# The recurrent mixer's input projection as three products of split weights and split input

## The reference

```python
def _recurrent_mixer(h, w_in, conv_w, conv_b, ga_w, ga_b, gx_w, gx_b, lam, w_out):
    u = h @ w_in                                   # 256x1024 by 1024x2048
    gate = jax.nn.gelu(u[..., :LRU_WIDTH])
    rec = _causal_depthwise_conv(u[..., LRU_WIDTH:], conv_w, conv_b)   # 4 taps
    rec = _rg_lru(rec, ga_w, ga_b, gx_w, gx_b, lam)
    return (gate * rec) @ w_out
```

## Time and profile before

| | |
|---|---|
| median of 3 runs | 1732.54 us (1730.82 to 1733.85) |
| profiled execution | 1730.7 us, span 1728.9 us |
| PE busy | 1460.7 us, 84% of the span |
| DVE busy | 869.5 us, 50% |
| ACT busy | 604.2 us, 35% |
| DMA | 408.72 MB, mean 236 GB/s |
| granted TensorE clock, mean | 0.939 of full |

### The profile page before, as it was taken

One profiled execution on the slowest core, in us unless ns is written; L12 is line 12 of the kernel. 1 busy time (PEld: TensorE's weight loads), 2 busy tenths in 40 slices (PEclk: granted clock), 3 DMA queues, 4 the chain that ended last, 5 costly groups with the idle time before them and its releaser, 6 DMA issues.

```text
span 1728.9 us, 26695 instructions
## 1 busy us (share of the span) xinstructions
PE 1460.7 (84%) x10828; PEld 1198.3 (69%) x10828; DVE 869.5 (50%) x1575; ACT 604.2 (35%) x1026; POOL 29.0 (2%) x40
## 2 busy tenths in 40 slices
PE   7986766678968665799989478999999999889998
PEld 6765432356644323599987358999899997679997
DVE  5663211157632111555556866555655556565555
ACT  5461100044611000444431254444444433454442
POOL 0000000000000000100000000000000000000000
PEclk9997987988979889899998789999999999999999
DMA  9725999994259999955554214555554562355520
GB/s 403 292 90 217 419 429 428 428 429 185 98 224 424 428 429 428 418 189 194 194 197 147 97 49 153 189 194 194 183 193 181 183 233 100 146 193 182 183 87 25
DMA packets 31025, 408.72 MB, mean 236 GB/s; under 512 B 3376, under 2 KB 5424, under 8 KB 6496
## 3 DMA queue, kind: packets, MB, share of 16 engines
q1 hardware_dynamic: 28496, 404.33, 58.9%
q10 hardware_dynamic: 2448, 3.24, 0.6%
HBM read 406.50 MB, written 1.06 MB: 236 GB/s over the span
## 4 chain that ended last, share of the span: by engine, by line
PE 58%; DMA 15%; issue 13%; DVE 11%; ACT 2%; POOL 1%; SPq 0%; DVEq 0%; POOLq 0%; ACTq 0%
DMA ring<-stream 15%; PE bank L1639 7%; PE bank L1643 7%; PE bank L1640 7%; PE bank L1670 7%; PE bank L614 5%; DVE cat L1880 3%; PE bank L1676 3%; PE bank L1947 3%; PE bank L1427 3%; PE bank L620 3%; PE bank L1445 3%; PE bank L594 2%; PE bank L386 1%; PE bank L1368 1%
## 5 line engine op out<-in xcount | busy, mean ns | idle before, releaser
L486 DVE TENSOR_TENSOR unit_lo<-ring,unit_hi 128x1024 fp32r<-128x1024 f32 x324 | 394.6, 1224 | 329.6 <-ACT unit_hi L481 329.4
L481 ACT ACTIVATE unit_hi<-ring 128x1024 fp32r<-128x1024 f32 x324 | 342.1, 1062 | 455.8 <-PE bank L1643 282.0
L1639 PE MATMUL bank<-hT_hi,unit_hi 128*128 128x256 f32 x1408 | 340.2, 282 | 0.9 <-DVE norm_lo L424 0.8
L1640 PE MATMUL bank<-norm_lo,unit_hi 128*128 128x256 f32 x1408 | 338.3, 279 | 0.0
L1639 PEld LDWEIGHTS bank<-hT_hi,unit_hi 128*128 128x128 f32 x1408 | 267.5, 190 | 5.6 <-issue 1.4
L1640 PEld LDWEIGHTS bank<-norm_lo,unit_hi 128*128 128x128 f32 x1408 | 264.9, 188 | 3.1
L1643 PE MATMUL bank<-hT_hi,unit_lo 128*128 128x256 f32 x1408 | 192.7, 279 | 0.0
L1427 PE MATMUL bank<-ring,work 128*32 128x256 f32 x1856 | 128.5, 429 | 64.7 <-DMA ring<-stream 53.7
L1643 PEld LDWEIGHTS bank<-hT_hi,unit_lo 128*128 128x128 f32 x1408 | 176.7, 188 | 0.0
L1427 PEld LDWEIGHTS bank<-ring,work 128*32 128x32 f32 x1856 | 63.6, 121 | 124.2 <-DMA ring<-stream 70.0
L1670 PE MATMUL bank<-unit_hi,act_lo 128*128 128x512 f32 x336 | 131.9, 393 | 0.0
(11 more groups left out here) (264 smaller groups left out, 1793.2 us busy)
## 6 DMA issues: line engine op xcount, KB each, us to landing
ring<-stream SPq DMA_DIRECT2D x183, 2048.0 KB, 12.8
work<-ahead SPq DMA_DIRECT2D x4, 2048.0 KB, 10.3
kept_slot<-ahead SPq DMA_DIRECT2D x2, 2048.0 KB, 23.8
ahead<-ahead SPq DMA_DIRECT2D x2, 2048.0 KB, 7.6
work<-spread ACTq DMA_DIRECT2D x2, 1024.0 KB, 12.6
x<-x_in SPq DMA_DIRECT2D x1, 1024.0 KB, 5.4
work<-final_rows ACTq DMA_DIRECT2D x2, 512.0 KB, 7.6
out<-x SPq DMA_DIRECT2D x2, 512.0 KB, 2.7
```

The costliest lines, as they stand in the source:

```text
L481: nc.scalar.activation(high_buf(name, u), raw_unit(name, u), ACT.Copy).then_inc(hi_done, 1)
L486: low = nc.vector.tensor_tensor(low_buf(name, u), raw_unit(name, u), high_buf(name, u).bitcast(F32), ALU.subtract)
L1639: nc.tensor.matmul(out, high[:, k, :], hT_hi[:, k, :], start=(k == 0), stop=False)
L1640: nc.tensor.matmul(out, high[:, k, :], norm_lo[:, k, :], start=False, stop=False)
```

## The change

The input projection of the last mixer becomes a stage of 16 units (`r_in`), each 128 output columns, repacked in the stream so that a unit is contiguous. Norm 8 takes the split form. `r_in` and `r_out` share three unit buffers, two in the slot that the experts had kept and one in the working area; the left side of `r_out` gets its own place, `rec_left`. The copies into the padded buffer go from VectorE to ScalarE, the clearing of it moves ahead of the log-sigmoid, the recurrent half now uses banks 4 to 7 and the Gelu half banks 0 to 3, and the splits of later units are placed between the other work of both engines. In `split_proj_pe` each `hT_hi` becomes `left_hi`.

```diff
+        kept_base = nc.sbuf_base
         kept_slot = sb("kept_slot", [P, SLOT])
...
-        few_hi, few_lo = part("few_hi", cat_base, 0, [2, UNIT]), part("few_lo", work_base, 12312, [2, UNIT])
+        rec_units = [[part(f"rec_unit{b}_{i}", base, at + i * UNIT, [UNIT]) for i in range(2)]
+                     for b, (base, at) in enumerate(((kept_base, 0), (kept_base, 2 * UNIT), (work_base, 12312)))]
+        rec_left = part("rec_left", work_base, 2048, [KD, T])
...
-        SPLIT_TURNS = ("n0", "cat_a", "n2", "n4", "cat_s", "n6", "n7", "n9")
+        SPLIT_TURNS = ("n0", "cat_a", "n2", "n4", "cat_s", "n6", "n7", "n8", "n9")
...
         STAGE_UNITS = {"a_in": 24, "a_out": 8, "c_in": 12, "c_out": 8, "ffn0": UNITS, "s_out": 8, "ffn1": UNITS,
-                       "ffn2": UNITS, "r_out": 8, "ffn3": UNITS}
+                       "ffn2": UNITS, "r_in": 16, "r_out": 8, "ffn3": UNITS}
...
         def depth(name):
-            return 2 if name == "r_out" else SPLIT
+            return 3 if name in ("r_in", "r_out") else SPLIT
 
         def high_buf(name, u):
-            return few_hi[:, u % 2, :] if name == "r_out" else unit_hi[:, (UNIT_BASE[name] + u) % SPLIT, :]
+            if name in ("r_in", "r_out"):
+                return rec_units[(u + (16 if name == "r_out" else 0)) % 3][0][:, :]
+            return unit_hi[:, (UNIT_BASE[name] + u) % SPLIT, :]
 
         def low_buf(name, u):
-            return few_lo[:, u % 2, :] if name == "r_out" else unit_lo[:, (UNIT_BASE[name] + u) % SPLIT, :]
+            if name in ("r_in", "r_out"):
+                return rec_units[(u + (16 if name == "r_out" else 0)) % 3][1][:, :]
+            return unit_lo[:, (UNIT_BASE[name] + u) % SPLIT, :]
...
         def split_high(act, name, u, it=0):
             n = START[name] + u // 4
             if u % 4 == 0:
                 act.wait_ge(slot_in[n % RING], 16 * (n // RING + 1) + 16 * it)
-            if u >= depth(name) or name in FOLLOWS_UNITS:
+            if u >= depth(name) or name in FOLLOWS_UNITS or name == "r_out":
                 act.wait_ge(unit_used, UNIT_BASE[name] + u - depth(name) + 1 + PASS_UNITS * it)
             nc.scalar.activation(high_buf(name, u), raw_unit(name, u), ACT.Copy).then_inc(hi_done, 1)
...
+            left_hi = rec_left if name == "r_out" else hT_hi
...
-        STAGE_AFTER = {"n2": "c_in", "n4": "ffn0", "n6": "ffn1", "n7": "ffn2", "n9": "ffn3"}
+        STAGE_AFTER = {"n2": "c_in", "n4": "ffn0", "n6": "ffn1", "n7": "ffn2", "n8": "r_in", "n9": "ffn3"}
...
         def r_mix_pe(pe):
-            n0 = START["r_in"]
+            turns = TURN_AT["n8"][0]
+
             def halves(g):
-                n = n0 + g // 2
-                if g % 2 == 0:
-                    loaded(pe, n)
-                if g >= 4:
-                    pe.wait_ge(rec_in, g - 3)
-                w = slot(n).rearrange("p (k c) -> p k c", k=KD)
                 for i in range(2):
-                    col = (g % 2) * 256 + i * P
+                    u, out = 2 * g + i, bank[(g + 4) % 8][:, i * T:(i + 1) * T]
+                    high = high_buf("r_in", u).rearrange("p (k c) -> p k c", k=KD)
+                    low = low_buf("r_in", u).rearrange("p (k c) -> p k c", k=KD)
+                    high_ready(pe, "r_in", u)
                     for k in range(KD):
-                        mm = nc.tensor.matmul(bank[g % 4][:, i * T:(i + 1) * T], w[:, k, col:col + P], hT[:, k, :],
-                                              start=(k == 0), stop=(k == KD - 1))
-                if g % 2:
-                    release(mm, n)
-                else:
-                    mm.then_inc(wide_done, 1)
+                        if u == 0 and k % 2 == 0:
+                            pe.wait_ge(*TURN_DONE[turns + k // 2])
+                        nc.tensor.matmul(out, high[:, k, :], hT_hi[:, k, :], start=(k == 0), stop=False)
+                        nc.tensor.matmul(out, high[:, k, :], norm_lo[:, k, :], start=False, stop=False)
+                    low_ready(pe, "r_in", u)
+                    for k in range(KD):
+                        mm = nc.tensor.matmul(out, low[:, k, :], hT_hi[:, k, :], start=False, stop=(k == KD - 1))
+                    mm.then_inc(unit_used, 1)
 
             for g in range(4):
                 halves(g)
             loaded(pe, n)
             for h in range(KD):
                 pe.wait_ge(rec_done, h + 1)
+                if h < 4:
+                    pe.wait_ge(rec_in, h + 1)
                 if h >= 4:
                     pe.wait_ge(rec_act, h - 1)
                 for m in range(2):
             split_proj_pe(pe, "r_out")
 
         def r_mix_act(act):
-            n0 = START["r_in"]
-
+            for j in range(4):
+                split_evac(act, 0, "n8", j)
+            split_high(act, "r_in", 2)
             act.wait_ge(rec_dve, 1)
             nc.scalar.activation(stat[:, 176:184], stat[:, 168:176], ACT.Exp).then_inc(rec_act, 1)
             act.wait_ge(rec_dve, 2)
             nc.scalar.activation(stat[:, 192:200], stat[:, 184:192], ACT.Ln).then_inc(rec_act, 1)
+            split_high(act, "r_in", 3)
+            act.wait_ge(pad_clear, 1)
+            for g in range(4):
+                act.wait_ge(unit_used, UNIT_BASE["r_in"] + 2 * g + 2)
+                nc.scalar.activation(pad_r[:, 2 * g:2 * g + 2, LW - 1:], bank[4 + g][:, :].rearrange("p (a b) -> p a b", a=2),
+                                     ACT.Copy).then_inc(rec_in, 1)
+                split_high(act, "r_in", 2 * g + 4)
+                if g < 3:
+                    split_high(act, "r_in", 2 * g + 5)
 
         def r_gelu_act(act, g):
-            if g % 2:
-                used(act, START["r_in"] + 2 + g // 2)
-            else:
-                act.wait_ge(wide_done, 5 + g // 2)
+            act.wait_ge(unit_used, UNIT_BASE["r_in"] + 2 * g + 10)
             nc.scalar.activation(gate_r[:, 2 * g:2 * g + 2, :].rearrange("p a b -> p (a b)"), bank[g][:, :],
                                  ACT.Gelu_apprx_tanh).then_inc(wide_act, 1)
 
                                      bias=gxb[:, h:h + 1]).then_inc(rec_act, 1)
             act.wait_ge(rec_dve, 3)
             nc.scalar.activation(tnh, dec, ACT.Tanh).then_inc(rec_act, 1)
+            split_high(act, "r_in", 11)
             act.wait_ge(rec_act, 11)
             nc.scalar.activation(dec, dec, ACT.Exp).then_inc(rec_act, 1)
+            split_high(act, "r_in", 12)
             act.wait_ge(rec_act, 12)
             nc.scalar.activation(spare, dec, ACT.Square).then_inc(rec_act, 1)
+            split_high(act, "r_in", 13)
             act.wait_ge(rec_dve, 4)
             nc.scalar.activation(tnh, tnh, ACT.Sqrt, scale=-1.0).then_inc(rec_act, 1)
+            for u in (14, 15):
+                split_high(act, "r_in", u)
             for g in range(3):
                 r_gelu_act(act, g)
-            for j in range(2):
-                split_high(act, "r_out", j)
+            for u in range(2):
+                split_high(act, "r_out", u)
             r_gelu_act(act, 3)
+            split_high(act, "r_out", 2)
             for j in range(4):
                 act.wait_ge(rec_out, j + 1)
-                nc.scalar.activation(hT_hi[:, 2 * j:2 * j + 2, :], tnh[:, 2 * j:2 * j + 2, :], ACT.Copy).then_inc(rec_hi, 1)
-            for u in range(2, 8):
+                nc.scalar.activation(rec_left[:, 2 * j:2 * j + 2, :], tnh[:, 2 * j:2 * j + 2, :], ACT.Copy).then_inc(rec_hi, 1)
+            for u in range(3, 8):
                 split_high(act, "r_out", u)
 
         def r_mix_dve(v):
-            n0 = START["r_in"]
             v.wait_ge(x_ready, 7)
+            for j in range(4):
+                split_evac(v, 1, "n8", j)
+            nc.vector.memset(pad_rf, 0.0).then_inc(pad_clear, 1)
+            split_low(v, "r_in", 2)
             e, u, ln, d, z = stat[:, 176:184], stat[:, 184:192], stat[:, 192:200], stat[:, 200:208], stat[:, 208:216]
             step(v, nc.vector.tensor_scalar(d, lam, -1.0, None, ALU.mult))
             nc.vector.tensor_tensor(stat[:, 168:176], d, lam, ALU.min).then_inc(rec_dve, 1)
             step(v, nc.vector.tensor_scalar(z, lam, 0.0, None, ALU.min))
             step(v, nc.vector.tensor_tensor(z, z, d, ALU.subtract))
             nc.vector.tensor_scalar(stat[:, C8:C8 + 8], z, 8.0, None, ALU.mult)
-            step(v, nc.vector.memset(pad_rf, 0.0))
             base = len(TAPS) - 1
             for g in range(4):
-                if g % 2:
-                    used(v, n0 + g // 2)
-                else:
-                    v.wait_ge(wide_done, 3 + g // 2)
-                nc.vector.tensor_copy(pad_r[:, 2 * g:2 * g + 2, LW - 1:],
-                                      bank[g][:, :].rearrange("p (a b) -> p a b", a=2)).then_inc(rec_in, 1)
+                split_low(v, "r_in", 2 * g + 3)
                 v.wait_ge(rec_in, g + 1)
                 for i in range(2 * LW):
                     j, k = i // 2, 2 * g + i % 2
```

(24 more changed lines are left out.)

## The result

The changed kernel took 1720.93 us (median of 4 runs, 1720.36 to 1722.87) against 1731.68 (4 runs, 1728.71 to 1733.85): a ratio of 0.9941, with a 95% interval of 0.9923 to 0.9959. In five more rounds the ratio was 0.9934 (0.9921 to 0.9947), 11.4 us. The forecast was 6.5 us less and 1726.0, with a range down to 1721.5.

What follows compares the result with a forecast made beforehand. TensorE was taken to bound the mixer up to 1496.7, VectorE to 1509.6, then TensorE. The output projection ending 8.2 us earlier, less 1.7 for clock, gave 6.5 us: 1726.0 us, range 1721.5 to 1731.0.

Steps and rivals of the forecast that it cites:

- TensorE's 2.80 us per unit: Input projection: 16 units make 44.8 us against 55.5, 10.7 us less TensorE work.
- the start: Norm 8 to unit 0: first matmul 4.50 us after the root's result, as in norm 9; costs 1.7 us.
- the gates: After unit 7: TensorE ends the first half at 1458.85, against 1462.14 before, and is free at 1466.1.
- the exposed table load: Gates, ScalarE: Sigmoid's load of 1.28 us leaves its idle time and stands behind high part 10, ending at 1461.8.
- the Sqrt: Second half, ScalarE: Sqrt from 1481.2 to 1483.1, 1.3 us later than before.
- the output chain: VectorE, after the second half: starts at 1486.5 and ends at 1504.0.
- its one wait for the left high part: Output chain: VectorE waits for left high part 0, queued on ScalarE behind high part 2 and ready at 1492.3.
- the wait of 0.45 for low part 4: Units 1 to 7: only low part 4, at 1449.5, is late for TensorE, by 0.45 us.
- Output projection: r_out: unit 2 starts at 1503.4, six units end at 1520.2, 8.2 us earlier, less 1.7 for clock.
- one such loss: r_out: one fall of TensorE's clock after its pauses, 1.7 us, kept in the sum.
- rival B: r_in's waits and r_out's pauses: clock falls cost 1.7 us each; six make it slower, 1736.2; chance 0.05.
- the forecast's own sign of being wrong: r_in: a granted clock below 1.00 there would show the forecast wrong.

Runs made afterwards that it cites:

- left_first: Changed kernel with ScalarE's left high part 0 ahead of r_out's high parts 1 and 2; ratio 0.9937 against the kernel before.
- half_less: Changed kernel without seven of the eight low-by-high matmuls in each of r_in's units 0 to 7; ratio 0.9918 against the kernel before.
- best_hold: Changed kernel, left high part 0 and low parts 2 earlier, constant products in pauses of norms 7, 8, 9 and r_out; 0.9927 against the kernel before.
- before_hold8: Kernel before with constant f32 products on TensorE in norm 8's two pauses; ratio 0.9983 against the kernel before.
- again: Changed kernel unaltered, in more rounds; ratio 0.9934 against the kernel before.
- r_out_alone: Kernel before with only the output projection's part of the change, r_in staying in plain f32; ratio 0.9982 against the kernel before.
- hold_clock: Changed kernel with seven constant f32 products on TensorE in the pause ahead of norms 7, 8 and 9; ratio 0.9935 against the kernel before.

## Why the prediction missed

**Right:** TensorE's 2.80 us per unit, the start (first matmul 5.20 us behind the POOL row's start, forecast 5.20), the gates at 1459.2 (1458.9), the exposed table load, the Sqrt at 1480.4 (1481.2), the output chain from 1485.6 (1486.5), its one wait for the left high part behind high part 2, its end at 1503.1 (1504.0), and unit 2 at 1502.3 (1503.4). The root of this execution lies 0.2 us earlier than the one that the forecast counts from, so the gates were 0.6 late and unit 2 was 0.9 early. The gates' closeness is in part luck: unit 1 should have started at 1438.8 and started at 1439.75, its unit 0 at half clock, and against that the wait of 0.45 for low part 4, which the forecast had, did not come.

**In the sum:** between the roots the profiles give 8.8 us where the forecast had 6.5. Of the 2.3 between them 0.9 is the earlier start of unit 2 (7.41 us ahead of before's, forecast 6.55) and 1.4 the clock in r_out.

**The step that failed first is in *Output projection*:** "I keep one such loss in the sum: 8.2 - 1.7". The clock stayed at 1.00 in r_out in both profiles of the changed kernel: 17.06 us for the six units against 18.44. So the term was 0 instead of 1.7, and its price is 1.4, since the six units take 17.06 at full clock and not 16.8. The pause before unit 2 was 2.80 us, forecast 3.2. Over all experiments a pause of 2.5 to 2.8 us before unit 2 was followed by full clock in five profiles and by a fall in two (left_first, half_less), one of 3.9 us by a fall in all five. I had rows for 3.31 and 3.92 and took the worse case. That the fall stayed away in the changed kernel is partly luck, since left_first had it behind the same 2.80.

**The second is in rival B and the sum:** "Plain f32 gave TensorE one unbroken stretch at clock 1.00". That was one execution. Rival B was right that the new form loses clock in r_in: it fell behind norm 8 in eight of its nine profiles, all but best_hold's, and the forecast's own sign of being wrong, a clock below 1.00 in r_in, was there. It had the price wrong, and it left the old form out. A fall behind norm 8 costs the old form 34.97 - 32.15 = 2.8 us up to the gates, because TensorE alone sets that stretch. It costs the new one 29.57 - 28.71 = 0.9: unit 1 starts 8.98 us behind the root with the clock held and 10.14 with a fall. The 1.2 between them is small because TensorE waits in unit 0 for the input's low parts anyway (2.84 us to its last eight matmuls with the clock held, against 1.87 in later units). Unit 4 gives 0.3 back, since with the clock held it waits for its low part on VectorE (starts of unit 1 in the changed kernel and in best_hold, whose roots lie at 1429.61 and 1432.69):

```profile
1439.75 0.28 PE L1955 MATMUL bank<-hT_hi,rec_unit 128*128 128x256 f32 x1
```

```profile
1441.67 0.28 PE L1966 MATMUL bank<-hT_hi,rec_unit 128*128 128x256 f32 x1
```

So the gain between the roots is 8.8 us (100.97 or 101.00 against 92.1) or 12.5 (104.66 against 92.1), by the execution of the kernel before, and the timed 10.2 and 11.4 lie between. That the falls of the old form make up this rest is argued from before_hold8's 2.9 us, its clock and its interval; it is not shown. A rival stands: norm 8's root came at 1430.6 us on average in the five profiles of the plain form and at 1429.8 in the nine of the new one, with single ones from 1426.6 to 1432.7, so some of the rest may lie ahead of the mixer. Behind it nothing was gained: norm 9's root to the last took 192.93 us in the changed kernel and 191.74 both before and in again.

**Small:** VectorE's period for two units was 5.30, not 5.55 (the low parts lie back to back at 1.13). The Sigmoids took 0.71 per pair instead of 0.86, since behind the table load they no longer waited for TensorE. They began 0.4 us later than forecast and the Tanh 0.5 earlier (1468.6, forecast 1469.1), of the 0.9 by which the output chain came earlier.

The Trainium skill's page "ScalarE: Activation LUTs" (section Step-by-step: what each stage is for) gives about 2.7 us for a table load including its drain. All six loads in the changed mixer took 1.28, and each began within 0.03 us of the end of the instruction before it, so no further 1.4 us shows. The Trainium skill's page "TensorE: Matmul & The Clock Gate" (Part 1) has the rule that idleness brings back the slow state. The falls read here all stand behind pauses of TensorE, which agrees with it, but equal pauses did not always bring one.

## What to carry to other kernels

An engine's loss of clock costs in full only where that engine is alone on the path: 2.8 us here in the old form, 0.9 in the new. Before pricing such a loss for the new schedule, price it for the old one, from more than one profiled execution. A profile may be a lucky one; compare its time with the spread of the runs, and take another if the gain at stake is of that size. When the profile names a releaser for a wait, check what else the instruction waits for and when that ended. Put the small operation that another engine waits for ahead of the large one that nobody waits for yet: that alone brought unit 2 forward by 2 us here, though a fall of the clock took most of it back.

## What the hardware showed unexpectedly

The same pause gave both outcomes: 3.31 us ahead of norm 8's transposes was followed by clock 1.00 in two profiles of the kernel before (and in r_out_alone) and by half clock in one, with the same code in front. In the new form the clock fell in all eight profiles in which not both pauses were filled: in five from about 3 us behind the root, in again, left_first and hold_clock from about 6. So whether the products of hold_clock, which filled the first pause alone, moved the fall is not shown. With both pauses filled (best_hold; at norm 7 hold_clock's first pause was enough) it stayed at 1.00 behind norms 7, 8 and 9. A fall behind norm 7 cost nothing to be seen (190.72 us to the next root with full clock, 190.63 to 190.74 with a fall); behind norm 9 the stretch to the last root took 191.7 to 191.9 or 192.8 to 192.9 us with falls, 191.8 without. The long ones are those whose half clock lasted beyond 9 us behind the root.
